# PEER block of a transformer kernel on one Trainium2 core: the first two weighted activations made ready under the last block of U

## The chip, the cores and the metric

The kernel runs on one NeuronCore of one Trainium2 chip. The metric is the device time of one execution in microseconds (us). Three timed runs of the kernel before gave 4199.46, 4199.56 and 4203.69 us: the median is 4199.56 us. The profile comes from a fourth execution.

## What is computed

Two layers of a two-stream trunk follow a first block. The change touches only the last part of each layer, a feed-forward block named PEER with 128 x 128 experts. It is called three times with 256 tokens: in layer 0 for both streams, in layer 1 for one. From the reference, cut:

```python
def peer_ffn(h, wq, sub_keys, eu, ev):
    ...
        q = (t @ wq).reshape(TOKEN_BLOCK, PEER_HEADS, 2, PEER_DK // 2)
        s = jnp.einsum("thpd,hpnd->thpn", q, sub_keys).astype(jnp.float32)
        st, it = lax.top_k(s, PEER_TOPK)
        ...
        best, pos = lax.top_k(cand, PEER_TOPK)
        e = jnp.take_along_axis(cidx, pos, axis=-1)
        g = jax.nn.softmax(best, axis=-1)
        u = jnp.take(eu, e, axis=0)
        act = jax.nn.gelu(jnp.einsum("thkd,td->thk", u, t).astype(jnp.float32), approximate=False)
        return jnp.einsum("thk,thkd->td", (g * act).astype(ev.dtype), jnp.take(ev, e, axis=0))
```

The kernel does not gather rows. It multiplies the tokens by all 16384 rows of `eu`, multiplies the result by a dense matrix of gates that is zero where an expert was not chosen, and multiplies that by all rows of `ev`.

## The kernel before

**Blocks and passes.** Weights come as blocks of 128 x 1024 numbers (512 KB). One call of PEER, a "pass" here, takes 8 blocks of `wq`, then 128 blocks of `eu` (U blocks, `u0 + c`), then 128 blocks of `ev` (V blocks, `v0 + c`), with c from 0 to 127. All blocks of the program come in one sequence through `ring`, which has NS = 4 places. SyncE starts the transfer of a block when the block four places earlier has been used: TensorE counts each block used in the semaphore `blocks_done`.

**Two parts of each number.** TensorE multiplies in a rounded format (fp32r), so each operand is split: the high part is its rounded copy, the low part the rest. For a block, ScalarE writes the high part (`high`, L1863, 128x1024, into `ring_hi`, 3 places) and then another engine the low part in the block's own place (`ring_lo`): GpSimd for U blocks below 48 (L1745), VectorE for the later U blocks (`low_up`, L2048) and for V blocks (`low`, L2063). A product takes three matmuls: high by high, high by low, low by high.

**U phase.** For U block c, `up` multiplies (24 matmuls of 256 columns, L1760 to L1762) into bank 4 + c % 4. ScalarE applies gelu (`gelu_late`, L1917 and L1919) and, behind it in the same function, writes the high part of the block that is three further: behind the gelu of U blocks 125, 126 and 127 it writes those of V blocks 0, 1 and 2. From c = 48 (`C0`) on, the gates are made beside this, four tokens at a time (a "quad", 64 of them): VectorE makes one-hot rows in `hotA` and `hotB` (L2019 to L2027), TensorE multiplies them (`build`, L1799) into banks 0 to 3, VectorE multiplies the rows of S that are there already (`gate`, L2036), and ScalarE stores the gates for the rows that are still to come (`keep_rest`, L1926); `gate_late` (L2042) multiplies such a row later. The last quad belongs to c = 126. S ends as the weighted activations, 128 rows of 128 x 256.

**V phase.** For each row c of S, ScalarE writes its high part (`weights`, L1938), VectorE its low part (`split`, L2056) and then the low part of V block c (`low`, L2063). `down` multiplies both (12 matmuls of 512 columns, L1813, L1815, L1817) into banks 0 to 3, where all 128 blocks add up. It waits for `v_lo` and `v_w`, which `low` and `split` count.

**Where the parts of S are kept.** `W_hi` and `W_lo` have four places each, in `H_r`. `H_r` also holds the high and low parts of the tokens, which every `up` reads. So nothing may be written there before the last U block has been multiplied: ScalarE and VectorE both wait for `blocks_done` at `n0 + v0`.

**Order.** Everything is written out by hand for each engine; each engine runs its instructions in that order, with semaphores between the engines. The loops of the V phase are hardware loops of 12 blocks a turn.

Of the kernel before, what the change touches and what calls it, by code (L numbers as in the profile page):

```python
# [9 lines left out]
F32R = mybir.dt.float32r  # L10
# [5 lines left out]
P = 128  # L16
D = 1024
KT = D // P
T = 256
# [13 lines left out]
PEER_H, TOPK, NK = 8, 16, 128  # L33
# [131 lines left out]
def build(nc, x, smalls, consts, mix_tables, tables, axial, w_in1, w_lru, w_br, w_o1, w_f1, w_f2, ada, w_in2,  # L165
          w_out2, w_q2, keys2, peer_u, peer_v, lam, out):
    ctx = ExitStack()
    with ctx:
# [3 lines left out]
        def pair_of(name, shape):  # L172

            at = (nc.sbuf_base + 31) // 32 * 32
            return sb(name, shape), nc.alloc_sbuf_tensor_at(name + "_r", shape, F32R, offset=at)
# [4 lines left out]
        H, H_r = pair_of("H", [P, KT, 2, T])  # L180
# [7 lines left out]
        arena_at = (nc.sbuf_base + 31) // 32 * 32  # L188
# [3 lines left out]
        blocks_done = ctx.enter_context(nc.semaphore("blocks_done"))  # L192
# [222 lines left out]
        A = Space(arena, n_arena)  # L415
# [64 lines left out]
        n0 = used[0]  # L480
# [80 lines left out]
        n0 = used[0]  # L561
# [132 lines left out]
        n0 = used[0]  # L694
# [109 lines left out]
        n0 = used[0]  # L804
# [116 lines left out]
        n0 = used[0]  # L921
# [70 lines left out]
        f = A.take(FFN_T, T)  # L992
        n0 = used[0]
# [58 lines left out]
        for l in range(LAYERS):  # L1052
# [85 lines left out]
            n0 = used[0]  # L1138
# [546 lines left out]
            for s in streams:  # L1685
# [3 lines left out]

                R = A.take(3, T)  # L1690
                S = A.take(NK, T)
                hotA = A.take(2, 4, P)
                hotB = A.take(2, 4, P)
                late = A.take(4, T)
                flat = S.rearrange("p c t -> p (c t)")
                work = Space(flat[:, 64 * T:], 64 * T)
# [11 lines left out]
                half = work.take(2, PEER_H, TOPK)  # L1708
                cand2 = S2.rearrange("p i k -> p (i k)").rearrange("p (h k) -> p h k", k=256)
                rows_, cols_, wts = (R[:, i, :] for i in range(3))  # L1710
                W_hi, W_lo = (H_r[:, 2 * i:2 * i + 2, :, :].rearrange("p a s t -> p (a s) t") for i in range(2))
                n0 = used[0]
                u0, v0 = 8, 8 + NK
                C0, QUADS = 48, T // 4
                first_row = [C0 + q * (NK - C0) // QUADS for q in range(QUADS)]

                def quads_at(c):

                    return [q for q in range(QUADS) if first_row[q] == c]

                def built(c):

                    return sum(f <= c for f in first_row)

                with Phase("keys_in", "by_q", "s_ps", "a_s", "v_read", "v_diff", "a_e", "v_found", "t_ps", "a_t",
# [5 lines left out]
                    def turns(it, n):  # L1731
                        return n if it is None else it * 12 + n
# [125 lines left out]
                    def _(act):  # L1858
                        def high(m, it=None):
                            arrived(act, n0 + m, None if it is None else it * 3)  # L1860
                            if m >= NH:
                                act.wait_ge(blocks_done, turns(it, n0 + m - NH + 1))
                            act.activation(ring_hi[:, m % NH, :], ring[:, (n0 + m) % NS, :], ACT.Copy).then_inc(a_hi, 1)  # L1863

                        def gelu(c, it=None):
                            act.wait_ge(blocks_done, turns(it, n0 + u0 + c + 1))
                            row = S[:, c, :] if it is None else S[:, bass.ds(it * 12 + c, 1), :].rearrange("p a t -> p (a t)")
                            act.activation(row, bank[4 + c % 4][:, 0:T], ACT.Gelu).then_inc(a_gelu, 1)
# [43 lines left out]
                        def gelu_late(c):  # L1912
                            t = 4 * built(c)
                            act.wait_ge(blocks_done, n0 + u0 + c + 1)
                            if c >= C0 + 4:
                                act.wait_ge(v_late, c - C0 - 3)
                            g = act.activation(late[:, c % 4, 0:t], bank[4 + c % 4][:, 0:t], ACT.Gelu)  # L1917
                            if t < T:
                                g = act.activation(S[:, c, t:], bank[4 + c % 4][:, t:T], ACT.Gelu)  # L1919
                            g.then_inc(a_gelu, 1)  # L1920
                            high(u0 + c + NH)

                        def keep_rest(q):
                            act.wait_ge(v_g, q + 1)
                            f = first_row[q]
                            act.activation(S[:, f:, 4 * q:4 * q + 4],  # L1926
                                           bank[q % 4][:, :].rearrange("p (t k) -> p k t", t=4)[:, f:, :],
                                           ACT.Copy).then_inc(a_rest, 1)

                        for c in range(C0, NK):  # L1930
                            gelu_late(c)
                            for q in quads_at(c):
                                keep_rest(q)
                        def weights(c, it=None):
                            if it is not None or c >= 4:
                                act.wait_ge(blocks_done, turns(it, n0 + v0 + c - 3))
                            w = S[:, c, :] if it is None else S[:, bass.ds(it * 12 + c, 1), :].rearrange("p a t -> p (a t)")
                            act.activation(W_hi[:, c % 4, :], w, ACT.Copy).then_inc(a_whi, 1)  # L1938

                        act.wait_ge(blocks_done, n0 + v0)  # L1940
                        act.wait_ge(v_g, QUADS)
                        act.wait_ge(v_late, NK - C0)
                        weights(0)
                        weights(1)
                        with act.Fori(0, 10) as it:
                            for c in range(12):
                                weights(2 + c, it)
# [7 lines left out]
                    def _(dve):  # L1955
# [27 lines left out]
                        for n in range(TT):  # L1983
                            dve.wait_ge(a_s, 4 * (n + 1))
                            cand = SC[n].rearrange("p i k -> p (i k)").rearrange("p (h k) -> p h k", k=256)
                            t, f = top[n], found[n]
# [43 lines left out]
                        def gate(q):  # L2030
                            f = first_row[q]
                            dve.wait_ge(g_ps, q + 1)
                            dve.wait_ge(a_gelu, f)
                            w = S[:, 0:f, 4 * q:4 * q + 4]
                            o = bank[q % 4][:, :].rearrange("p (t k) -> p k t", t=4)[:, 0:f, :]
                            dve.tensor_tensor(w, w, o, ALU.mult).then_inc(v_g, 1)  # L2036

                        def gate_late(c):
                            t = 4 * built(c)
                            dve.wait_ge(a_gelu, c + 1)  # L2040
                            dve.wait_ge(a_rest, built(c))
                            dve.tensor_tensor(S[:, c, 0:t], S[:, c, 0:t], late[:, c % 4, 0:t], ALU.mult).then_inc(v_late, 1)  # L2042
# [8 lines left out]
                        def split(c, it=None):  # L2051
                            if it is not None or c >= 4:
                                dve.wait_ge(blocks_done, turns(it, n0 + v0 + c - 3))
                            w = S[:, c, :] if it is None else S[:, bass.ds(it * 12 + c, 1), :].rearrange("p a t -> p (a t)")
                            dve.wait_ge(a_whi, turns(it, c + 1))
                            dve.tensor_tensor(W_lo[:, c % 4, :], w, W_hi[:, c % 4, :].bitcast(F32),  # L2056
                                              ALU.subtract).then_inc(v_w, 1)

                        def low(c, it=None):
                            m = v0 + c  # L2060
                            dve.wait_ge(a_hi, turns(it, m + 1))
                            slot = (n0 + m) % NS
                            dve.tensor_tensor(ring_lo[:, slot, :], ring[:, slot, :], ring_hi[:, m % NH, :].bitcast(F32),  # L2063
                                              ALU.subtract).then_inc(v_lo, 1)
# [7 lines left out]
                        for c in range(C0, NK):  # L2072
                            quads = quads_at(c)
                            for q in quads:
                                gate(q)
                                if q + 2 < QUADS:
                                    hit_keys(q + 2)
                            if c + 2 < NK:
                                low_up(c + 2)
                            for q in quads:  # L2080
                                if q + 2 < QUADS:
                                    weigh_keys(q + 2)
                            if c > C0:
                                gate_late(c - 1)
                        gate_late(NK - 1)
                        dve.wait_ge(blocks_done, n0 + v0)

                        with dve.Fori(0, 10) as it:
                            for c in range(12):
                                split(c, it)  # L2090
                                low(c, it)
                        for c in range(120, NK):
                            split(c)
                            low(c)
                used[0] += 8 + 2 * NK
# [157 lines left out]
```

## Time and profile before

| | |
|---|---|
| median of three runs | 4199.56 us |
| time of the profiled execution | 4205.55 us |
| its span, first to last instruction | 4201.9 us |
| mean granted TensorE clock over the span | 0.949 of full |
| TensorE matmul busy | 3852.6 us (92%) |
| VectorE busy | 2364.2 us (56%) |
| ScalarE busy | 1688.7 us (40%) |
| GpSimd busy | 782.0 us (19%) |

Busy time is time with an instruction running; the granted clock is the share of TensorE's full clock that the chip let through. Between span and time of the same execution lie 3.65 us that have no instruction. In the rows further below, times count from the first instruction.

### The profile page before, as it was taken

How to read it: one execution, taken by the hardware profiler on the slowest of the kernel's cores; microseconds unless marked ns; L12 is line 12 of the kernel's file. 1: busy time of each engine (PE TensorE's matmuls, PEld its weight loads, DVE VectorE, ACT ScalarE, POOL GpSimd, SP SyncE). 2: the span in 40 equal slices, each digit the busy share in tenths (PEclk: the TensorE clock that was granted, in tenths of full speed). 3: DMA queues.
4: the chain of work that ended last, by engine and by line, in shares of the span. 5: the costliest groups of instructions: out<-in, count | busy, mean ns of one | idle time of the engine just before them, and what ended most of it. 6: DMA issues, size and time to landing. Idle time of an engine off the chain costs nothing. (4 is left out here: it accounts for less than half of the span.)

```text
span 4201.9 us, 67550 instructions
## 1 busy us (share of the span) xinstructions
PE 3852.6 (92%) x23930; PEld 3376.7 (80%) x23930; DVE 2364.2 (56%) x4653; ACT 1688.7 (40%) x2999; POOL 782.0 (19%) x315
## 2 busy tenths in 40 slices
PE   7997788978978999999989999999879799999998
PEld 7984378966655999988879999888767699998887
DVE  5002322226451878965547889655555377896555
ACT  3542202313332544444545444454433244444544
POOL 5750004600002830000018400000000085000000
PEclk9997899998889999999999999999988899999999
DMA  5565644632102544456645545566421154445664
GB/s 185 177 200 179 210 153 135 179 107 76 59 1 79 162 146 149 148 167 193 193 152 165 150 146 146 165 192 193 151 83 52 54 164 150 150 147 161 193 192 150
DMA packets 168448, 614.95 MB, mean 146 GB/s; under 512 B 18592, under 2 KB 20000, under 8 KB 167968
## 3 DMA queue, kind: packets, MB, share of 16 engines
q1 hardware_dynamic: 168224, 611.88, 47.7%
q8 instruction: 150, 2.46, 0.2%
q14 instruction: 74, 0.61, 0.0%
HBM read 610.76 MB, written 1.05 MB: 146 GB/s over the span
## 5 line engine op out<-in xcount | busy, mean ns | idle before, releaser
L1863 ACT ACTIVATE ring_hi<-ring 128x1024 fp32r<-128x1024 f32 x792 | 839.3, 1060 | 616.2 <-DMA ring<-in_peer_v 510.2
L1760 PE MATMUL bank<-H_r,ring_hi 128*128 128x256 f32 x3264 | 947.5, 290 | 64.3 <-POOL ring_r L1745 62.8
L1761 PE MATMUL bank<-H_r,ring_hi 128*128 128x256 f32 x3264 | 927.2, 284 | 0.0
L1762 PE MATMUL bank<-H_r,ring_r 128*128 128x256 f32 x3264 | 926.6, 284 | 0.0
L1745 POOL TENSOR_TENSOR ring_r<-ring,ring_hi 128x1024 fp32r<-128x1024 f32 x168 | 456.1, 2729 | 1429.3 <-ACT ring_hi L1863 1428.6
L1760 PEld LDWEIGHTS bank<-H_r,ring_hi 128*128 128x128 f32 x3264 | 629.8, 193 | 72.3 <-POOL ring_r L1745 46.4
L1761 PEld LDWEIGHTS bank<-H_r,ring_hi 128*128 128x128 f32 x3264 | 630.5, 193 | 0.0
L1762 PEld LDWEIGHTS bank<-H_r,ring_r 128*128 128x128 f32 x3264 | 629.5, 193 | 0.0
L1813 PE MATMUL bank<-ring_hi,H_r 128*128 128x512 f32 x1536 | 476.6, 392 | 12.2 <-DVE ring_r L2063 12.1
L1815 PE MATMUL bank<-ring_r,H_r 128*128 128x512 f32 x1536 | 475.5, 391 | 0.0
L1817 PE MATMUL bank<-ring_hi,H_r 128*128 128x512 f32 x1536 | 475.5, 391 | 0.0
L2063 DVE TENSOR_TENSOR ring_r<-ring,ring_hi 128x1024 fp32r<-128x1024 f32 x384 | 467.9, 1219 | 0.0
L290 PE MATMUL bank<-H_r,ring_hi 128*128 128x256 f32 (+1 forms) x1464 | 457.9, 313 | 0.0
L2056 DVE TENSOR_TENSOR H_r<-arena,H_r 128x256 fp32r<-128x256 f32 x384 | 163.4, 426 | 452.4 <-ACT H_r L1938 441.1
L280 POOL TENSOR_TENSOR ring_r<-ring,ring_hi 128x1024 fp32r<-128x1024 f32 x133 | 318.9, 2401 | 503.0 <-ACT ring_hi L274 502.3
L1813 PEld LDWEIGHTS bank<-ring_hi,H_r 128*128 128x128 f32 x1536 | 290.0, 189 | 73.8 <-DVE ring_r L2063 13.6
L1815 PEld LDWEIGHTS bank<-ring_r,H_r 128*128 128x128 f32 x1536 | 290.1, 189 | 60.6
L1817 PEld LDWEIGHTS bank<-ring_hi,H_r 128*128 128x128 f32 x1536 | 290.0, 189 | 60.7
L289 PE MATMUL bank<-H_r,ring_hi 128*128 128x256 f32 x1064 | 305.0, 287 | 28.7 <-POOL ring_r L280 28.7
L2048 DVE TENSOR_TENSOR ring_r<-ring,ring_hi 128x1024 fp32r<-128x1024 f32 x240 | 293.1, 1221 | 65.6 <-ACT ring_hi L1863 64.5
L291 PE MATMUL bank<-H_r,ring_r 128*128 128x256 f32 x1064 | 304.0, 286 | 0.0
L290 PEld LDWEIGHTS bank<-H_r,ring_hi 128*128 128x128 f32 x1464 | 289.8, 198 | 14.2
(318 smaller groups left out, 5300.1 us busy)
## 6 DMA issues: line engine op xcount, KB each, us to landing
ring<-in_peer_u SPq DMA_DIRECT2D x384, 512.0 KB, 3.6
ring<-in_peer_v SPq DMA_DIRECT2D x384, 512.0 KB, 3.6
ring<-in_w_in SPq DMA_DIRECT2D x135, 512.0 KB, 3.6
ring<-in_ada SPq DMA_DIRECT2D x96, 512.0 KB, 4.7
ring<-in_w_f SPq DMA_DIRECT2D x72, 512.0 KB, 3.7
ring<-in_w_br SPq DMA_DIRECT2D x24, 512.0 KB, 3.6
ring<-in_w_q SPq DMA_DIRECT2D x24, 512.0 KB, 3.6
ring<-in_w_out SPq DMA_DIRECT2D x16, 512.0 KB, 3.6
```

Of the source, the lines that this page charges most:

```text
L280: eng.tensor_tensor(ring_lo[:, slot, :], ring[:, slot, :], ring_hi[:, m % NH, :].bitcast(F32), ALU.subtract).then_inc(lows, 1)
L289: pe.matmul(o, hi[:, k], x_hi(kt), start=(kt == 0), stop=False)
L290: pe.matmul(o, hi[:, k], x_lo(kt), start=False, stop=False)
L1745: pool.tensor_tensor(ring_lo[:, slot, :], ring[:, slot, :], ring_hi[:, m % NH, :].bitcast(F32), ALU.subtract).then_inc(p_lo, 1)
L1760: pe.matmul(o, hi[:, k], x_hi_[:, kt, :], start=(kt == 0), stop=False)
L1761: pe.matmul(o, hi[:, k], x_lo_[:, kt, :], start=False, stop=False)
L1762: mm = pe.matmul(o, lo[:, k], x_hi_[:, kt, :], start=False, stop=(kt == KT - 1))
L1813: pe.matmul(bank[2 * t + e][:, :], w_hi, hi[:, v], start=start, stop=False)
L1815: pe.matmul(bank[2 * t + e][:, :], w_hi, lo[:, v], start=False, stop=False)
L1817: mm = pe.matmul(bank[2 * t + e][:, :], w_lo, hi[:, v], start=False, stop=stop)
L1863: act.activation(ring_hi[:, m % NH, :], ring[:, (n0 + m) % NS, :], ACT.Copy).then_inc(a_hi, 1)
L2063: dve.tensor_tensor(ring_lo[:, slot, :], ring[:, slot, :], ring_hi[:, m % NH, :].bitcast(F32), ALU.subtract).then_inc(v_lo, 1)
```

## The change

`W_hi` and `W_lo` move from `H_r` to the place in `arena` where `hotA` and `hotB` lie (2 x 1024 numbers a partition, the same size as 2 x 4 x 256). The one-hot rows are no longer needed once the last quad has been multiplied and gated. ScalarE writes the high parts of rows 0 and 1 ahead of the gelu of U block 127, behind a wait for `g_ps` and `v_g` at 64. VectorE writes the low parts of rows 0 and 1 and of V blocks 0 and 1 ahead of `gate_late(127)`. The waits for `blocks_done` at `n0 + v0` on both engines are gone. VectorE's loop then runs over c from 2 to 13 in its first turn.

```diff
                 S = A.take(NK, T)
+                W_hi, W_lo = (nc.alloc_sbuf_tensor_at(f"w_{part}{l}{s}", [P, 4, T], F32R,
+                                                      offset=arena_at + 4 * (A.at + i * 4 * T))
+                              for i, part in enumerate(("high", "low")))
                 hotA = A.take(2, 4, P)
                 hotB = A.take(2, 4, P)
...
-                W_hi, W_lo = (H_r[:, 2 * i:2 * i + 2, :, :].rearrange("p a s t -> p (a s) t") for i in range(2))
...
-                        for c in range(C0, NK):
-                            gelu_late(c)
-                            for q in quads_at(c):
-                                keep_rest(q)
                         def weights(c, it=None):
...
-                        act.wait_ge(blocks_done, n0 + v0)
-                        act.wait_ge(v_g, QUADS)
+                        for c in range(C0, NK):
+                            if c == NK - 1:
+                                act.wait_ge(g_ps, QUADS)
+                                act.wait_ge(v_g, QUADS)
+                                weights(0)
+                                weights(1)
+                            gelu_late(c)
+                            for q in quads_at(c):
+                                keep_rest(q)
                         act.wait_ge(v_late, NK - C0)
-                        weights(0)
-                        weights(1)
                         with act.Fori(0, 10) as it:
...
                             if c > C0:
                                 gate_late(c - 1)
+                        for c in range(2):
+                            split(c)
+                            low(c)
                         gate_late(NK - 1)
-                        dve.wait_ge(blocks_done, n0 + v0)
 
                         with dve.Fori(0, 10) as it:
-                            for c in range(12):
+                            for c in range(2, 14):
                                 split(c, it)
                                 low(c, it)
-                        for c in range(120, NK):
+                        for c in range(122, NK):
                             split(c)
                             low(c)
```

In the changed kernel the line numbers are a few off those of before. ScalarE, end of the U phase in the first pass, before: the gelu of U block 126 (from bank6), the high part of V block 1, the last `keep_rest` (bank3), the gelu of U block 127 (bank7), the high part of V block 2, `weights` of rows 0 and 1, and the loop's first instructions, which are row 2.

```order
L1917 ACTIVATE arena<-bank6 128x256
L1863 ACTIVATE ring_hi<-ring 128x1024
L1926 ACTIVATE arena<-bank3 128x2x4
L1917 ACTIVATE arena<-bank7 128x256
L1863 ACTIVATE ring_hi<-ring 128x1024
L1938 ACTIVATE H_r_50<-arena 128x256 x2
L1945 UNCONDITIONAL_BRANCH
```

The same place of the changed kernel:

```order
L1919 ACTIVATE arena<-bank6 128x256
L1865 ACTIVATE ring_hi<-ring 128x1024
L1928 ACTIVATE arena<-bank3 128x2x4
L1936 ACTIVATE w_high00_10652<-arena 128x256 x2
L1919 ACTIVATE arena<-bank7 128x256
L1865 ACTIVATE ring_hi<-ring 128x1024
L1948 UNCONDITIONAL_BRANCH
```

Two `weights` moved ahead of the last gelu and of the high part of V block 2. VectorE, the same place, before: the last `gate`, then `gate_late` of rows 125, 126 and 127, the loop, and in it `split(0)` and `low(0)`.

```order
L2036 TENSOR_TENSOR arena<-arena,bank3 128x126x4
L2042 TENSOR_TENSOR arena<-arena 128x252
L2042 TENSOR_TENSOR arena<-arena 128x256 x2
L2088 UNCONDITIONAL_BRANCH
L2088 ISA
L2055 REGISTER_ALU
L2056 ISA
L2056 TENSOR_TENSOR H_r_50<-arena,H_r_50 128x256
L2061 REGISTER_ALU
L2063 TENSOR_TENSOR ring_r_49<-ring,ring_hi 128x1024
```

The changed kernel, from `gate_late` of row 125 on:

```order
L2045 TENSOR_TENSOR arena<-arena 128x252
L2045 TENSOR_TENSOR arena<-arena 128x256
L2059 TENSOR_TENSOR w_low00_10653<-arena,w_high00_10652 128x256
L2066 TENSOR_TENSOR ring_r_49<-ring,ring_hi 128x1024
L2059 TENSOR_TENSOR w_low00_10653<-arena,w_high00_10652 128x256
L2066 TENSOR_TENSOR ring_r_49<-ring,ring_hi 128x1024
L2045 TENSOR_TENSOR arena<-arena 128x256
L2093 UNCONDITIONAL_BRANCH
```

Two pairs of `split` and `low` moved out of the loop and ahead of `gate_late(127)`. TensorE, GpSimd and SyncE have the same instructions in the same order as before.

## Rows read from the trace of the kernel before

**Rows 1.** The page's costliest groups: first matmul of `down`, busy, mean, idle before.

```profile
L1813 PE MATMUL bank<-ring_hi,H_r 128*128 128x512 f32 x1536 | 476.6, 392 | 12.2 <-DVE ring_r L2063 12.1
```

**Rows 2.** Timeline of PE, pass 1: start, duration, what, [idle before <-releaser].

```profile
1818.05 1.22 PE L1813 MATMUL bank<-ring_hi,H_r 128*128 128x512 f32 x2 [3.93 <-DVE ring_r L2063]
...
1826.10 0.61 PE L1813 MATMUL bank<-ring_hi,H_r 128*128 128x512 f32 x2
...
1828.82 0.61 PE L1813 MATMUL bank<-ring_hi,H_r 128*128 128x512 f32 x2
```

**Rows 3.** Timeline of ACT, pass 1, around the end of the U phase.

```profile
1812.13 1.06 ACT L1863 ACTIVATE ring_hi<-ring 128x1024 fp32r<-128x1024 f32 x1 [0.46 <-DMA ring<-in_peer_v]
1813.09 0.16 ACT L1926 ACTIVATE arena<-bank 128x8 f32<-128x8 f32 x1
...
1815.89 1.01 ACT L1938 ACTIVATE H_r<-arena 128x256 fp32r<-128x256 f32 x3
```

**Rows 4.** Timeline of DVE, the same stretch.

```profile
1813.35 0.43 DVE L2042 TENSOR_TENSOR arena<-arena 128x256 f32<-128x256 f32 x1 [3.84 <-ACT arena L1926]
...
1816.44 0.43 DVE L2056 TENSOR_TENSOR H_r<-arena,H_r 128x256 fp32r<-128x256 f32 x1 [1.44 <-ACT H_r L1938]
1816.78 1.22 DVE L2063 TENSOR_TENSOR ring_r<-ring,ring_hi 128x1024 fp32r<-128x1024 f32 x1
```

**Rows 5.** Timeline of PE, passes 2 and 3: first matmuls of V blocks 0 and 2.

```profile
2668.08 1.22 PE L1813 MATMUL bank<-ring_hi,H_r 128*128 128x512 f32 x2 [4.01 <-DVE ring_r L2063]
...
2676.11 0.61 PE L1813 MATMUL bank<-ring_hi,H_r 128*128 128x512 f32 x2
...
3827.79 1.22 PE L1813 MATMUL bank<-ring_hi,H_r 128*128 128x512 f32 x2 [3.87 <-DVE ring_r L2063]
...
3836.17 0.62 PE L1813 MATMUL bank<-ring_hi,H_r 128*128 128x512 f32 x2
```

**Rows 6.** Timeline of ACT, passes 2 and 3: the last `keep_rest`.

```profile
2662.46 0.17 ACT L1926 ACTIVATE arena<-bank 128x8 f32<-128x8 f32 x1
...
3822.31 0.17 ACT L1926 ACTIVATE arena<-bank 128x8 f32<-128x8 f32 x1
```

**Rows 7.** Timeline of DVE, passes 2 and 3: `gate_late(126)` and `split(0)` of each.

```profile
2662.73 0.42 DVE L2042 TENSOR_TENSOR arena<-arena 128x256 f32<-128x256 f32 x1 [3.28 <-ACT arena L1926]
...
2666.47 0.43 DVE L2056 TENSOR_TENSOR H_r<-arena,H_r 128x256 fp32r<-128x256 f32 x1 [1.52 <-ACT H_r L1938]
...
3822.58 0.42 DVE L2042 TENSOR_TENSOR arena<-arena 128x256 f32<-128x256 f32 x1 [3.25 <-ACT arena L1926]
...
3826.17 0.43 DVE L2056 TENSOR_TENSOR H_r<-arena,H_r 128x256 fp32r<-128x256 f32 x1 [1.37 <-ACT H_r L1938]
```

**Rows 8.** Stretches: length; busy of PE, PEld, DVE, ACT, POOL; clock, DMA share, GB/s.

```profile
1425.00:1515.00 90.00, 83.77 (x686) 82.38 (x685) 72.16 (x214) 45.45 (x64) 80.28 (x30) 1.00 0.55 163
1818.05:1823.38 5.33, 5.33 (x13) 4.17 (x14) 2.89 (x4) 0.00 (x0) 0.00 (x0) 0.50 0.01 2
1823.38:2169.00 345.62, 345.56 (x1525) 285.76 (x1523) 195.06 (x250) 170.72 (x250) 0.00 (x0) 1.00 0.64 192
3130.70:3134.10 3.40, 3.40 (x19) 3.40 (x18) 1.78 (x5) 0.00 (x0) 0.00 (x0) 0.50 0.09 36
```

**Rows 9.** Waits of PE, 1425 to 1515: total, times, longest.

```profile
PE bank L1760 <- POOL ring_r L1745: 6.2, 7, 1.3
```

**Rows 10.** Timeline of PE at two other gaps.

```profile
3129.87 0.63 PE L1177 MATMUL bank<-CS,arena 128*128 128x128 f32 x4 [2.00 <-ACT arena L1225]
...
3877.43 0.73 PE L1813 MATMUL bank<-ring_hi,H_r 128*128 128x512 f32 x2 [0.30 <-DVE ring_r L2063]
```

**Rows 11.** Timeline of DVE, pass 1: low part of V block 5.

```profile
1832.03 1.22 DVE L2063 TENSOR_TENSOR ring_r<-ring,ring_hi 128x1024 fp32r<-128x1024 f32 x1
```

**Rows 12.** Weight loads by line: duration min/median/max in ns; `down` and `build`.

```profile
L1813 PEld LDWEIGHTS bank<-ring_hi,H_r x1536: 186/188/333, 1818.1 to 4178.1; 128*128 128x128 f32 x192
L1799 PEld LDWEIGHTS bank<-arena x1536: 186/192/338, 1524.9 to 3817.8; 128*128 128x128 f32 x192
```

## Prediction

> **What bounds the kernel now.** I read the page first: TensorE is busy nearly all the time, so only places where it stands still, or where its clock is low, can be worth anything. The group of the first matmul of `down` shows 12.2 us of idle time ahead of it, almost all of it waiting for VectorE's low part of a block, 12.1 us [rows 1]. The timeline of PE says where that is: once at each change from U to V, 3.93, 4.01 and 3.87 us [rows 2, 5], with 0.30 us left for one hiccup in the third V phase [rows 10]. Next, how long a V block takes: block 1 starts to be followed by block 2 at 1826.10 and block 3 at 1828.82, so 2.72 us a block [rows 2]. But the first two V blocks of pass 1 took from 1818.05 to 1826.10, 8.05 us where two blocks should take 5.44. The windows say why: the granted clock was 0.50 from 1818.05 to 1823.38, that is 1.2 GHz, and 1.00 (2.4 GHz) from there on to the end of the pass [rows 8]. So each change of phase costs twice: the standstill, and a V block at half clock behind it.
>
> Why the standstill lasts 3.9 us is read from the timelines of ACT and DVE. The last U block's matmuls end at 1818.05 - 3.93 = 1814.12. Only then do the last gelu and the high part of V block 2 run; the `weights` start at 1815.89 [rows 3], `split(0)` at 1816.44, `low(0)` at 1816.78, and PE goes on at 1818.05 [rows 4, 2]. From `weights` to `split` is 0.55 us, from `split` to PE 1.61 us. None of this needs the last U block except for the place it writes to. ScalarE's last `keep_rest` starts at 1813.09 and VectorE's `gate_late(126)` at 1813.35, behind it [rows 3, 4]: from there on both are free.
>
> **The change part by part.** Nothing is added or taken away but the two waits. Three passes, and in each two `weights`, two `split` and two `low` move to the front.
>
> *The new start of V.* In pass 1 `keep_rest` runs from 1813.09 for 0.16 us. I let `weights(0)` start 0.11 behind its start, since each engine's next instruction begins some 0.05 to 0.1 us ahead of the end of the last (the high part of V block 1 from 1812.13 for 1.06 us, `keep_rest` at 1813.09 [rows 3]). That is 1813.20, and `split(0)` 0.55 later is 1813.75; `gate_late(126)`, ahead of it on VectorE, is just over by then (1813.35 + 0.43). `split(0)` stood at 1816.44, so it comes 2.69 us earlier, and PE with it: 1815.36 in place of 1818.05. Pass 2: `keep_rest` 2662.46 [rows 6], `weights(0)` 2662.57, `split(0)` 2663.12 where `gate_late(126)` (2662.73 + 0.42) ends too; it stood at 2666.47 [rows 7], 3.35 us. Pass 3: 3822.31, 3822.42, 3822.97, against 3826.17: 3.20 us. Together 9.24 us. Left are standstills of 3.93 - 2.69 = 1.24, 4.01 - 3.35 = 0.66 and 3.87 - 3.20 = 0.67 us. Pass 1 keeps more because `keep_rest` stands there behind the high part of V block 1, which waited for its DMA until 1812.13 [rows 3].
>
> *The clock.* The trace has no standstill of this kind at this place, so I bound it. From below: in 1425 to 1515, also under U blocks, PE stood still seven times for GpSimd, 6.2 us in all and up to 1.3 us at a time [rows 9], and the granted clock was 1.00 throughout [rows 8]. From above: a standstill of 2.00 us ended at 3129.87 [rows 10], and the clock was 0.50 from 3130.7 to 3134.1 [rows 8]. My 1.24, 0.66 and 0.67 us lie under 1.3, the first of them closely, so I take it that the clock holds in all three. What comes back is the excess of the first two V blocks over 5.44 us: 8.05 - 5.44 = 2.61 in pass 1, 2676.11 - 2668.08 - 5.44 = 2.59 in pass 2, 3836.17 - 3827.79 - 5.44 = 2.94 in pass 3 [rows 2, 5]: 8.14 us.
>
> The Trainium skill, TensorE: Matmul & The Clock Gate, section "Part 1: The HAM clock gate", says that the count of matmuls at the low clock after a pause varies between runs of one kernel (6, 11 or 14 were seen), since the monitor is not tied to the kernel. Here the trace shows some 12 to 13 a time. By that rule, at 0.2 us a matmul, three places would hold 3.6 to 8.4 us in the timed runs and not 8.14 for certain, and the sum would be 12.8 to 17.6 us, an estimate from that page.
>
> *ScalarE's new wait.* `weights(0)` waits for the last quad's product and gate, and the gelu of U block 127 is queued behind it. `keep_rest`, one instruction ahead, waits for the same gate already, so the wait costs nothing; and two `weights` of about 0.34 us each (three took 1.01 [rows 3]) are over at 1813.9, before the last U block ends at 1814.12. No cost.
>
> *VectorE's new order.* `gate_late(127)`, and behind it `weights(2)` and `split(2)`, now stand behind two `low`. From the start of `low(0)` PE is 1.27 us away (1816.78 to 1818.05 [rows 2, 4]). VectorE needs 1.22 + 0.43 + 1.22 + 0.43 = 3.30 us to the end of `gate_late(127)`, about 0.15 to hand over, 0.55 from `weights(2)` to `split(2)`, and 1.61 to PE: 6.61, or 5.34 us after PE starts V block 0. Counted in whole durations, with no overlap, that is still ahead of 5.44, when PE comes to V block 2; with the overlaps of 0.1 us an instruction it is about 0.5 us ahead. No cost, but the cover is thin: a delay past it is paid in full.
>
> *The ring.* The pause used to let V block 3 land. It is still asked for when the last U block ends, and PE comes to it 0.66 + 3 x 2.72 = 8.8 us later. Block 4 is asked for when block 0 is done, as in the steady phase, where the low part of V block 5 is ready at 1832.03 + 1.22 = 1833.25 [rows 11] and PE comes to it at 1828.82 + 2 x 2.72 = 1834.26: 1.0 us to spare. The transfers keep the DMA engines busy 0.64 of the time at 192 GB/s [rows 8], so the V phase runs at TensorE's pace and an earlier start becomes an earlier end. The one late transfer in the third V phase cost 0.30 us [rows 10].
>
> *Sum.* 9.24 + 8.14 = 17.4 us, three changes of phase together. The profiled execution would take 4205.55 - 17.4 = 4188.2 us. The median of the runs stands 6.0 us under that execution (4199.56); I take the same saving there: 4182.2, so 4182 us.
>
> **The rivals.**
> *A, the pause goes, the half clock stays.* The clock could still fall behind 1.24 us, or behind the shorter ones; the timeline has nothing between 1.3 and 2.00 to tell, and other standstills of up to 1.3 us held. Then only 9.24 us come back: 4190.3 us. If it falls in pass 1 alone, 4184.8.
> *B, the wait moves on.* PE waits at V block 2 for the longer queue on VectorE, or later for the ring, and the half clock follows there. Against it: 0.5 to 1.0 us of cover. It must lose over 9 us in three passes to hide the gain, 3 us each: a wait of about 0.5 us and a slow block of 2.6 us each time. About 4191 to 4199, say 4196 us.
> *C, slower: the new place of the parts costs TensorE.* In the V phase it loads its weights from `arena`, where ScalarE and VectorE read and write too. There are 3 x 1536 = 4608 such loads. If each matmul took 3.8 ns more, the gain would be gone (17.4 / 4608); from 5.6 ns on the kernel is slower by 0.2%. The rows have a load from `arena` at 192 ns in `build` against 188 ns from `H_r` in `down` [rows 12]: 4 ns more. But a matmul is started every 227 ns (2.72 / 12), which covers a load of 192. With 8 ns exposed it would cost 36.9 - 17.4 = 19.5 us: 4219 us.
> *D, nothing happens,* because something on ScalarE or VectorE still ends after the last U block. The order of the changed kernel speaks against it: `split(0)` and `low(0)` stand ahead of all that needs that block.
>
> **How the numbers follow.** Forecast, both parts come back: 0.77. A, in part or whole: 0.12. B and D: 0.07. C: 0.04. Time of the likeliest: 4182. Downward the range takes in standstills gone to nothing (11.81 + 8.14 = 19.95 us, 4179.6) and some 1.5 us of scatter: 4178. Upward it takes in all of A: 4191. That leaves 1 in 10 out above. The likeliest alone has 4179 to 4186. A measurement of this kernel can tell about 0.2% from no change, 8.4 us. The forecast and two thirds of A are beyond that, for 9.24 is close to it: faster 0.85. The rest of A with B and D: same 0.11. C: slower 0.04.
>
> **What the profile of the changed kernel would show.** At each change from U to V a gap of 0.6 to 1.3 us ahead of the first matmul of `down`, in place of 3.9; `weights` twice between the last `keep_rest` and the last gelu; pairs of first V blocks in 5.4 us, not 8; granted clock 1.00 across the change. Against me would be: the clock at 0.50 behind the short gap (A), a wait of `down` for VectorE at V block 2 (B), matmuls of `down` over 227 ns apart (C), or `weights(0)` after the last U block (D). The likeliest error is in the clock of pass 1.

## The result, and the profile after

The changed kernel is slower: 4215.27 us median against 4203.16 us for the kernel before over 13 runs each, a ratio of 1.0031 with a 95% interval from 1.0022 to 1.0039. Forecast was 4182 us. The profiled execution took 4217.31 us with a span of 4213.8 us; before it was 4205.55 and 4201.9.

At the change from U to V everything went as forecast. Timeline of PE in the changed kernel, the first matmuls of `down` in the three passes (L1815 is the line that was L1813, answering to [rows 2, 5]); the second and third rows are the first matmuls of V blocks 1 and 2 of pass 1:

```profile
1810.48 0.74 PE L1815 MATMUL bank<-ring_hi,w_high 128*128 128x512 f32 x2 [1.05 <-DVE ring_r L2066]
...
1813.39 0.63 PE L1815 MATMUL bank<-ring_hi,w_high 128*128 128x512 f32 x2
...
1816.19 0.63 PE L1815 MATMUL bank<-ring_hi,w_high 128*128 128x512 f32 x2
...
2669.28 0.73 PE L1815 MATMUL bank<-ring_hi,w_high 128*128 128x512 f32 x2 [0.61 <-DVE ring_r L2066]
...
3833.59 0.74 PE L1815 MATMUL bank<-ring_hi,w_high 128*128 128x512 f32 x2 [0.61 <-DVE ring_r L2066]
```

The standstills are 1.05, 0.61 and 0.61 us, 2.27 in place of 11.81. V block 0 runs from 1810.48 to 1813.39, 2.91 us, and with block 1 it takes 5.71 us to 1816.19, where before the two took 8.05 us in pass 1, 5.33 of them at half clock [rows 2, 8]. Windows of 8 us across the three changes of phase show the clock at 1.00:

```profile
1808.00:1816.00 8.00, 6.95 (x36) 5.71 (x36) 5.80 (x10) 4.27 (x9) 0.00 (x0) 1.00 0.53 155
2667.00:2675.00 8.00, 7.39 (x39) 6.10 (x39) 5.47 (x9) 4.07 (x9) 0.00 (x0) 1.00 0.56 172
3831.00:3839.00 8.00, 7.39 (x40) 6.19 (x39) 5.58 (x9) 4.38 (x9) 0.00 (x0) 1.00 0.59 160
```
ACT (ScalarE) and then DVE (VectorE), the same stretch, answering to [rows 3, 4]:

```profile
1808.27 0.16 ACT L1928 ACTIVATE arena<-bank 128x8 f32<-128x8 f32 x1
1808.32 0.71 ACT L1936 ACTIVATE w_high<-arena 128x256 fp32r<-128x256 f32 x2
1809.47 0.38 ACT L1919 ACTIVATE arena<-bank 128x256 f32<-128x256 f32 x1 [0.43 <-PE bank L1764]
```

```profile
1808.53 0.43 DVE L2045 TENSOR_TENSOR arena<-arena 128x256 f32<-128x256 f32 x1 [3.71 <-ACT arena L1928]
1808.87 0.42 DVE L2059 TENSOR_TENSOR w_low<-arena,w_high 128x256 fp32r<-128x256 f32 x1
1809.21 1.22 DVE L2066 TENSOR_TENSOR ring_r<-ring,ring_hi 128x1024 fp32r<-128x1024 f32 x1
...
1811.81 0.42 DVE L2045 TENSOR_TENSOR arena<-arena 128x256 f32<-128x256 f32 x1
1813.11 0.42 DVE L2059 TENSOR_TENSOR w_low<-arena,w_high 128x256 fp32r<-128x256 f32 x1 [0.88 <-ACT w_high L1936]
1813.45 1.22 DVE L2066 TENSOR_TENSOR ring_r<-ring,ring_hi 128x1024 fp32r<-128x1024 f32 x1
```

Both `weights` are over before the last gelu; `low(0)` ends at 1810.43 and PE starts. The low part of V block 2 is over at 1814.67; PE comes to it at 1816.19.

The loss is in what looks like no event at all. Windows of the steady phases, kernel before and then the changed kernel: the first row lies in the V phase of pass 1, the second in the U phase. In the V phase every PE instruction is a matmul of `down`, so length over count is the step from one to the next.

```profile
1850.00:2140.00 290.00, 290.00 (x1281) 240.14 (x1280) 166.50 (x214) 145.25 (x215) 0.00 (x0) 1.00 0.64 193
1600.00:1790.00 190.00, 190.00 (x1614) 190.00 (x1614) 172.92 (x277) 82.84 (x202) 0.00 (x0) 1.00 0.48 148
```

```profile
1850.00:2140.00 290.00, 290.00 (x1244) 233.48 (x1243) 162.27 (x208) 140.78 (x207) 0.00 (x0) 1.00 0.62 187
1600.00:1790.00 190.00, 190.00 (x1613) 190.00 (x1613) 173.10 (x277) 82.84 (x202) 0.00 (x0) 1.00 0.49 147
```

PE is busy 100%, the clock is 1.00 and PE waits for nothing, in both. But 290 us hold 1281 matmuls before and 1244 after: 226.4 against 233.1 ns (both some 0.3 ns low, since a matmul that reaches over an edge is counted whole). The U phase has not changed (1614 and 1613 instructions in 190 us). No matmul record is missing: the page counts all 1536 of each line of `down`, before and after. The page says the same in its mean duration and hides it well:

```profile
L1815 PE MATMUL bank<-ring_hi,w_high 128*128 128x512 f32 x1536 | 483.8, 396 | 2.8 <-DVE ring_r L2066 2.5
```

The wait went from 12.2 to 2.8 us [rows 1], the mean duration from 392 to 396 ns, although 392 had three V blocks at half clock in it. At 6.7 ns for each of 3 x 1536 = 4608 matmuls the V phases lose 30.9 us. With 9.5 us of standstill and 8.1 us of half clock won, that is 13.3 us more; the spans differ by 11.9 and the medians by 12.1. The close fit is in part chance: in the profiled execution of the changed kernel the first U block started 5.2 us earlier (1335.6 against 1340.8 us), and the three U phases took some 4 us longer, though the change touches neither.

### The profile page after: what moved, and what is told of

Read it like the earlier page. It is cut to its first block and busy times, and to the rows that moved or that the text cites. A ratio compares the mean times of both kernels' runs of the same rounds, so it can differ in the third digit from the quotient of the medians.

```text
span 4213.8 us, 67544 instructions
## 1 busy us (share of the span) xinstructions
PE 3872.1 (92%) x23930; PEld 3369.8 (80%) x23930; DVE 2369.5 (56%) x4653; ACT 1689.5 (40%) x2999; POOL 781.0 (19%) x315
## 3 DMA queue, kind: packets, MB, share of 16 engines
HBM read 610.76 MB, written 1.05 MB: 145 GB/s over the span
## 5 line engine op out<-in xcount | busy, mean ns | idle before, releaser
L1762 PE MATMUL bank<-H_r,ring_hi 128*128 128x256 f32 x3264 | 948.4, 291 | 65.7 <-POOL ring_r L1747 64.6
L1764 PE MATMUL bank<-H_r,ring_r 128*128 128x256 f32 x3264 | 927.3, 284 | 0.0
L1762 PEld LDWEIGHTS bank<-H_r,ring_hi 128*128 128x128 f32 x3264 | 630.6, 193 | 73.7 <-POOL ring_r L1747 46.4
L1764 PEld LDWEIGHTS bank<-H_r,ring_r 128*128 128x128 f32 x3264 | 629.9, 193 | 0.0
L1815 PE MATMUL bank<-ring_hi,w_high 128*128 128x512 f32 x1536 | 483.8, 396 | 2.8 <-DVE ring_r L2066 2.5
L1817 PE MATMUL bank<-ring_r,w_high 128*128 128x512 f32 x1536 | 482.9, 395 | 0.0
L1819 PE MATMUL bank<-ring_hi,w_low 128*128 128x512 f32 x1536 | 482.9, 395 | 0.0
L2059 DVE TENSOR_TENSOR w_low<-arena,w_high 128x256 fp32r<-128x256 f32 x384 | 163.4, 426 | 469.4 <-ACT w_high L1936 469.4
L1815 PEld LDWEIGHTS bank<-ring_hi,w_high 128*128 128x128 f32 x1536 | 288.2, 188 | 74.0 <-DVE ring_r L2066 5.0
L1819 PEld LDWEIGHTS bank<-ring_hi,w_low 128*128 128x128 f32 x1536 | 288.8, 188 | 69.8
L1817 PEld LDWEIGHTS bank<-ring_r,w_high 128*128 128x128 f32 x1536 | 288.8, 188 | 69.5
```

What stands on the lines that cost most here:

```text
L1762: pe.matmul(o, hi[:, k], x_hi_[:, kt, :], start=(kt == 0), stop=False)
L1764: mm = pe.matmul(o, lo[:, k], x_hi_[:, kt, :], start=False, stop=(kt == KT - 1))
L1815: pe.matmul(bank[2 * t + e][:, :], w_hi, hi[:, v], start=start, stop=False)
L1817: pe.matmul(bank[2 * t + e][:, :], w_hi, lo[:, v], start=False, stop=False)
L1819: mm = pe.matmul(bank[2 * t + e][:, :], w_lo, hi[:, v], start=False, stop=stop)
```

## The experiments

**place_only.** The placing alone: the kernel before with the parts where the changed kernel has them, order and waits as they were.

```diff
                 S = A.take(NK, T)
+                W_hi, W_lo = (nc.alloc_sbuf_tensor_at(f"w_{part}{l}{s}", [P, 4, T], F32R,
+                                                      offset=arena_at + 4 * (A.at + i * 4 * T))
+                              for i, part in enumerate(("high", "low")))
                 hotA = A.take(2, 4, P)
...
-                W_hi, W_lo = (H_r[:, 2 * i:2 * i + 2, :, :].rearrange("p a s t -> p (a s) t") for i in range(2))
```

> The kernel before, its order and its waits untouched; only W_hi and W_lo lie in arena, at the place where the changed kernel has them. Theory P (the place alone slows the matmuls of down): the step from one matmul of down to the next is 231 to 236 ns instead of 227, some 10 us a pass and 31 us in all, on top of the old standstills: about 4234 us against 4203. Rival T (the matmuls are slower because of the new order: engines now work at other times beside TensorE): steps stay at 227 ns and the time is that of before, 4203 us.

Measured: 4240.23 us against 4205.57, ratio 1.0081 (1.0055 to 1.0106). Window of the V phase of pass 1:

```profile
1850.00:2140.00 290.00, 290.00 (x1245) 233.65 (x1244) 162.24 (x208) 141.26 (x208) 0.00 (x0) 1.00 0.63 187
```

290 / 1245 = 232.9 ns. The place makes the step from one matmul of `down` to the next longer, with the old order of all engines. Rival T, the new order as the cause, has fallen.

**first_two.** The order nearly alone: the changed kernel, with only rows 0 and 1 in `arena`. From row 2 on the parts are in `H_r` again, so ScalarE's wait for the last U block comes back, but behind the last gelu.

```diff
-                W_hi, W_lo = (nc.alloc_sbuf_tensor_at(f"w_{part}{l}{s}", [P, 4, T], F32R,
...
+                W_first = [nc.alloc_sbuf_tensor_at(f"w_{part}{l}{s}", [P, 2, T], F32R,
+                                                   offset=arena_at + 4 * (A.at + i * 4 * T))
+                           for i, part in enumerate(("high", "low"))]
+                W_rest = [H_r[:, 2 * i:2 * i + 2, :, :].rearrange("p a s t -> p (a s) t") for i in range(2)]
+
+                def part_of(i, c, it=None):
+                    return W_first[i][:, c, :] if it is None and c < 2 else W_rest[i][:, c % 4, :]
...
                         act.wait_ge(v_late, NK - C0)
+                        act.wait_ge(blocks_done, n0 + v0)
```

> The changed kernel, but only rows 0 and 1 have their parts in arena; from row 2 on they lie in H_r as in the kernel before, written after the last U block is done. Under any of the theories of place (P1, P2) all but two V blocks a pass run at 227 ns and the short standstill stays: 4203 - 9.9 - 8.1, about 4185 us. Under T the steps stay at 231 to 236 ns and it takes about 4215 us.

Measured: 4184.11 us, ratio 0.9954 (0.9937 to 0.9970). Two changes of phase in the timeline of PE, and the window:

```profile
1821.84 0.73 PE L1820 MATMUL bank<-ring_hi,w_high 128*128 128x512 f32 x2 [0.95 <-DVE ring_r L2072]
...
2668.97 0.73 PE L1820 MATMUL bank<-ring_hi,w_high 128*128 128x512 f32 x2 [0.61 <-DVE ring_r L2072]
```

```profile
2720.00:2980.00 260.00, 260.00 (x1149) 215.29 (x1148) 148.91 (x192) 130.67 (x192) 0.00 (x0) 1.00 0.65 193
```

260 / 1149 = 226.3 ns, short standstills, 21 us less than before. So the two halves of the change can be had apart, and the half that the forecast was about is worth about what it said.

**h_plus64.** What is it about the place? `W_hi` and `W_lo` in the memory of `H`, 64 bytes further on. The kernel is otherwise that of before.

```diff
...
+            places[name] = at
...
-                W_hi, W_lo = (H_r[:, 2 * i:2 * i + 2, :, :].rearrange("p a s t -> p (a s) t") for i in range(2))
+                W_hi, W_lo = (nc.alloc_sbuf_tensor_at(f"w_{part}{l}{s}", [P, 4, T], F32R,
+                                                      offset=places["H"] + 64 + 4 * i * 4 * T)
+                              for i, part in enumerate(("high", "low")))
```

> The kernel before, with W_hi and W_lo still in the memory of H, but 64 bytes further: H begins at byte 61568 of a partition, a multiple of 128, while the place in arena is byte 216768, which is 64 past a multiple of 128. Theory P1 (it is the start address modulo 128): steps of 231 to 236 ns here too, about 4234 us. Rival P2 (it is the region, arena against H, or what else is read and written there): steps of 227 ns, 4203 us.

**after_plus64.** The changed kernel with the parts 64 bytes further on, `late` too.

```diff
-        n_arena = 36612
+        n_arena = 36624
...
-                                                      offset=arena_at + 4 * (A.at + i * 4 * T))
+                                                      offset=arena_at + 64 + 4 * (A.at + i * 4 * T))
...
                 hotB = A.take(2, 4, P)
+                A.take(16)
```

> The changed kernel with W_hi and W_lo 64 bytes further, at byte 216832, a multiple of 128; late moves up by the same 64 bytes. Theory P1: steps return to 227 ns, the V phases lose their 31 us, and the time is 4215 - 31 = 4184 us. Rival P2: nothing changes, 4215 us.

Measured: h_plus64 4232.84 us, ratio 1.0067 (1.0042 to 1.0091); after_plus64 4215.77 us, 1.0027 (1.0013 to 1.0041). Windows, h_plus64 first:

```profile
1850.00:2140.00 290.00, 290.00 (x1244) 233.52 (x1243) 161.80 (x208) 141.08 (x208) 0.00 (x0) 1.00 0.63 188
```

```profile
1850.00:2140.00 290.00, 290.00 (x1245) 233.18 (x1244) 161.34 (x208) 141.75 (x208) 0.00 (x0) 1.00 0.64 188
```

Both are slow, 233.1 and 232.9 ns. P2, the region as the cause, falls by the first, for nothing but 64 bytes was changed; P1, the address modulo 128, falls by the second, at a multiple of 128 that should have been fast. The addresses (bytes in a partition; those of the ring counted back from `H` by the sizes of the tensors) suggested the next question: `ring` 16512, `ring_hi` 32896 and `H` 61568 are alike modulo 4096, and with them the parts of before; the slow places 216768, 216832 and 61632 are not like them modulo 256, nor modulo 512.

**sweep_a, sweep_b, sweep_c.** The edit of h_plus64 with another shift in each pass, (128, 256, 512), (32, 384, 2048) and (96, 160, 224).

> The kernel before, W_hi and W_lo in the memory of H, another shift in each pass: 128, 256 and 512 bytes. With a shift of 0 the step of down is 227 ns, with 64 bytes it was 233 on average, and at the place in arena (192 past a multiple of 512, as H plus 64) it was 233 with the same alternation of 231 and 236. Theory M (what counts is the start address modulo 512, the length of the 128 numbers that one weight load reads): 128 and 256 bytes are slow, above 230 ns, 512 bytes is fast, 227 ns. Rival N (any tensor that isn't H_r itself is slow, whatever its address): all three passes are slow. Rival K (modulo 128): all three are fast.

> The same with shifts of 32, 384 and 2048 bytes. Theory M: 32 and 384 are slow, above 230 ns a step, 2048 is fast, 227 ns. Rival N: all slow. Rival K: only 32 is slow.

> The kernel before, W_hi and W_lo in the memory of H shifted by 96, 160 and 224 bytes in passes 1, 2 and 3. Theory M2 says all three are slow, 232 to 233 ns a step, since only multiples of 256 have been fast (0, 256, 512, 2048) and 32, 64, 128 and 384 slow. A theory by which only distances of 32 to 128 cost would have 224 near 227 ns.

Windows of the V phases of passes 1, 2 and 3, of sweep_a, sweep_b and sweep_c in turn:

```profile
1850.00:2140.00 290.00, 290.00 (x1250) 235.15 (x1249) 162.53 (x209) 142.02 (x208) 0.00 (x0) 1.00 0.61 188
2720.00:2980.00 260.00, 260.00 (x1149) 215.29 (x1148) 149.74 (x192) 130.56 (x191) 0.00 (x0) 1.00 0.64 192
3880.00:4130.00 250.00, 250.00 (x1104) 207.01 (x1103) 143.66 (x184) 125.56 (x184) 0.00 (x0) 1.00 0.63 193
```

```profile
1850.00:2140.00 290.00, 290.00 (x1244) 233.50 (x1244) 161.17 (x208) 141.94 (x208) 0.00 (x0) 1.00 0.61 187
2720.00:2980.00 260.00, 260.00 (x1120) 210.83 (x1119) 145.31 (x187) 127.44 (x188) 0.00 (x0) 1.00 0.62 188
3880.00:4130.00 250.00, 250.00 (x1101) 205.88 (x1100) 143.48 (x184) 124.80 (x183) 0.00 (x0) 1.00 0.64 192
```

```profile
1850.00:2140.00 290.00, 290.00 (x1240) 233.63 (x1239) 161.30 (x208) 140.76 (x206) 0.00 (x0) 1.00 0.61 187
2720.00:2980.00 260.00, 260.00 (x1116) 209.31 (x1115) 144.62 (x186) 127.00 (x186) 0.00 (x0) 1.00 0.61 187
3880.00:4130.00 250.00, 250.00 (x1073) 201.28 (x1072) 138.70 (x179) 121.54 (x178) 0.00 (x0) 1.00 0.63 187
```

Length over count gives, by shift in bytes:

| shift | 0 | 32 | 64 | 96 | 128 | 160 | 224 | 256 | 384 | 512 | 2048 |
|---|---|---|---|---|---|---|---|---|---|---|---|
| ns a step | 226.4 | 233.1 | 233.1 | 233.9 | 232.0 | 233.0 | 233.0 | 226.3 | 232.1 | 226.4 | 227.1 |

Each of these kernels was timed once: 4217.36, 4219.41 and 4236.91 us, with one, two and three slow passes. Of the shifts tried, the multiples of 256 are fast and no other is. N (any other tensor is slow) and K (modulo 128) have fallen. M (modulo 512) put 256 among the slow ones and missed; the period is 256 bytes.

**all_plus64.** The kernel before, with everything 64 bytes later.

```diff
+        pad = sb("pad", [P, 16])
         ring, ring_lo = pair_of("ring", [P, NS, SLOT])
```

> The kernel before with 64 bytes of padding ahead of ring, so that ring, ring_hi and H (with W_hi and W_lo in it) all begin 64 bytes later. Theory M in its relative form (what counts is where the stationary operand lies against the moving one, modulo 512): down keeps 227 ns a step and the time is that of before, about 4204 us. In its absolute form (128 past a multiple of 512 is the good address): 233 ns and some 31 us more.

One run: 4207.46 us, against 4205.53 for the kernel before. 290 us of the V phase hold 1281 matmuls, as before:

```profile
1850.00:2140.00 290.00, 290.00 (x1281) 240.22 (x1280) 166.11 (x214) 145.74 (x214) 0.00 (x0) 1.00 0.63 193
```

So it is a distance between tensors and not an address in itself.

**ring_apart.** The same padding between `ring` and `ring_hi`, so that `ring` alone is 64 bytes off; `arena` moves with `H`.

> The kernel before with 64 bytes of padding between ring and ring_hi, so that ring_hi and H (with W_hi and W_lo) begin 192 past a multiple of 256 while ring, with the low parts of the blocks, stays at 128. Theory M2 (TensorE is slow while its stationary and its moving operand differ in their start address modulo 256): of the 12 matmuls of a V block the four with the low part of the block (middle line) are slow, some 233 ns a step, the eight with ring_hi keep 227: about 229 ns on average, 10 us more in three passes; in the U phase the steps at the low part of the block become slower too, if that phase feels it at all. Rival S (what counts is where W lies against S in arena, which ScalarE and VectorE read meanwhile): nothing changes against the kernel before, since H and arena move together: 227 ns in all steps.

One run: 4201.69 us, beside 4209.72 for one run of the kernel before. Windows of the V and the U phase of pass 1, then the lines of `down` in the first of them (duration min/median/max in ns; 389 in all three before):

```profile
1850.00:2140.00 290.00, 290.00 (x1257) 235.92 (x1256) 163.79 (x210) 142.16 (x210) 0.00 (x0) 1.00 0.63 189
1600.00:1790.00 190.00, 190.00 (x1634) 190.00 (x1633) 174.25 (x279) 84.02 (x205) 0.00 (x0) 1.00 0.49 149
```

```profile
L1814 PE MATMUL bank<-ring_hi,H_r x419: 388/390/396, 1850.1 to 2139.9; 128*128 128x512 f32 x140
L1816 PE MATMUL bank<-ring_r,H_r x418: 393/394/395, 1850.6 to 2139.2; 128*128 128x512 f32 x140
L1818 PE MATMUL bank<-ring_hi,H_r x420: 387/393/398, 1849.7 to 2139.7; 128*128 128x512 f32 x140
```

290 / 1257 = 230.7 ns: slower, though the distance from `W` (`W_hi` and `W_lo`) to the weighted activations is unchanged. Rival S has fallen, and the distance to `ring` counts. But M2 was too simple. It had 229 ns, with the two lines of `ring_hi` untouched; many of their matmuls are longer too, up to 396 and 398. The slow matmul is not told by its own two operands alone. And the U phase got faster: 1634 instructions in 190 us, where all other kernels so far had 1612 to 1615.

**arena_first.** The changed kernel, with `arena` allocated right behind `H` and the small tensors behind `arena`, so that `W_hi` begins at 212096, like `ring` modulo 256.

```diff
         H, H_r = pair_of("H", [P, KT, 2, T])
+        n_arena = 36612
+        arena_at = (nc.sbuf_base + 31) // 32 * 32
+        arena = sb("arena", [P, n_arena])
...
-        n_arena = 36612
...
-        arena_at = (nc.sbuf_base + 31) // 32 * 32
-        arena = sb("arena", [P, n_arena])
```

> The changed kernel, but arena is laid right behind H and the small tensors behind arena: hotA, and with it W_hi, then begins at byte 212096, 128 past a multiple of 512, as ring, ring_hi and H do. Nothing else differs. Theory M: down runs at 227 ns and the time is 4215 - 31 = 4184 us, as much as when only the first two rows lie in arena. Rival N, or a theory by which reads and writes of arena by other engines cost TensorE: 233 ns, 4215 us. Other phases may shift by a few us either way, since their tensors in arena move too.

Measured: 4186.54 us against 4205.53, ratio 0.9952 (0.9939 to 0.9964).

```profile
1850.00:2140.00 290.00, 290.00 (x1281) 240.15 (x1280) 166.32 (x213) 145.86 (x214) 0.00 (x0) 1.00 0.64 193
```

226.4 ns, with the parts in `arena` throughout and as far from the weighted activations as in the changed kernel. Reads and writes of `arena` by the other engines cost TensorE nothing that shows.

**h_apart64, h_apart128.** Since ring_apart had sped up the U phase: arena_first with `H`, which holds the tokens' parts, moved alone by 64 or 128 bytes; `arena` moves by 256 bytes in all, so that `W` stays like `ring` modulo 256. The edit for 64 bytes, against arena_first; for 128 both paddings are 32 numbers.

```diff
+        pad = sb("pad", [P, 16])
         H, H_r = pair_of("H", [P, KT, 2, T])
+        pad2 = sb("pad2", [P, 48])
```

> arena_first with H alone 64 bytes further; W_hi, W_lo, ring and ring_hi stay alike modulo 256. In ring_apart, where ring lay 64 bytes off ring_hi and H, a V block was slower but the steps of the U phase fell from 119.7 to 118.3 ns. Theory U1 (any distance between TensorE's operands costs, in U as in V; ring_apart was a chance): the U phase gets slower than 119.7, the V phase stays at 227, time above 4187. Theory U2 (with 256 columns, where the next weights are loaded in almost the whole step, a distance helps): U steps of 118 ns or less, V at 227, some 13 us less than arena_first, 4174 us.

> The same with H 128 bytes further, half of 256. U1: U steps above 119.7 ns, time above 4187. U2: below, about 4174 us.

Measured: h_apart64 4159.07 us against 4199.61, ratio 0.9909 (0.9879 to 0.9938); h_apart128 4179.38, 0.9941 (0.9918 to 0.9964). Windows of V (pass 2) and U (pass 1), h_apart64 and then h_apart128:

```profile
2720.00:2980.00 260.00, 260.00 (x1149) 215.37 (x1148) 149.28 (x192) 130.21 (x192) 0.00 (x0) 1.00 0.65 193
1600.00:1790.00 190.00, 190.00 (x1634) 190.00 (x1633) 174.31 (x279) 83.88 (x205) 0.00 (x0) 1.00 0.51 149
```

```profile
2720.00:2980.00 260.00, 260.00 (x1149) 215.29 (x1148) 148.70 (x192) 130.55 (x192) 0.00 (x0) 1.00 0.65 193
1600.00:1790.00 190.00, 190.00 (x1609) 190.00 (x1608) 172.39 (x277) 82.09 (x201) 0.00 (x0) 1.00 0.49 147
```

The V phase is as fast as before. (Counted from the starts in the traces, a step of `up` is 119.8 ns before and 117.8 in ring_apart, where the expectation has 119.7 and 118.3.) At 64 bytes the window of the U phase holds 1634 in place of 1612 to 1615 instructions; at 128 it holds 1609, a little slower. U2 is right for 64, though more was won than its 13 us. At 128 neither is right: the window is no faster, against U2, but the time did not rise above 4187 us, against U1, and by its interval it can't be told from arena_first.

h_apart64 is the fastest of all, 4159 us, and by the ratios it lies 0.43%, some 18 us, under arena_first. From the first to the last start of the first line of `up` (L1762 and L1764), the traces have in pass 1 472.7 us for arena_first (1345.4 to 1818.1) and 466.8 for h_apart64 (1330.4 to 1797.2), the 8 blocks of `wq` included; in pass 2 it is 473.9 and 465.2, in pass 3 472.8 and 465.9. That is 21.5 us less in three passes, so the U phases alone can account for the 18. At 128 bytes the same stretches are together within 2 us of arena_first. Products of other phases also read `ring` against `H`; their share was not taken apart.

## Why the prediction was wrong

*The standstill.* Right. Forecast 1.24, 0.66 and 0.67 us left, measured 1.05, 0.61, 0.61; won 9.5 us for 9.24. In pass 1 `keep_rest` stood 1.16 us ahead of the end of the U phase and not 1.03 as before (1809.43 - 1808.27, 1814.12 - 1813.09), which is most of the difference. The time that the saving was taken from was 3.6 us low: the median of the first three runs, 4199.56, against 4203.16 of thirteen. That alone would not have left the range.

*The clock.* Right. It stayed at 1.00 in all three passes. The first two V blocks of pass 1 took 5.71 us where two blocks at the new step take 5.60; so nearly all of the 8.14 us came back. The prediction takes 6, 11 and 14 matmuls at the low clock from the section "Part 1: The HAM clock gate" of the Trainium skill's page "TensorE: Matmul & The Clock Gate"; the page gives these counts for the start of a kernel, not for a pause inside one. The eight kernels here with the old order have 24 such pauses at the change from U to V, of 3.7 to 4.9 us, and behind every one 8 to 14 matmuls of `down` ran at half clock. first_two has both terms without the third and lies 21 us under the kernel before where the sum was 17.4; its interval, 0.30% to 0.63%, holds that sum.

*ScalarE's wait, VectorE's order, the ring.* Right: no cost that shows. VectorE had 1.5 us to spare at V block 2 where I had counted 0.1 to 0.5, so B had nothing to stand on.

*The place.* Here it failed. The step was under rival C: "a matmul is started every 227 ns, which covers a load of 192". I priced the new place by how long a weight load lasts, found 4 ns in the row of another line, and let the matmul hide it. Neither is what happened. The loads are as long as before, a median of 188 ns in all three lines of `down`, as this pair shows for the middle one, before and after (1850 to 2140):

```profile
L1815 PEld LDWEIGHTS bank<-ring_r,H_r x426: 187/188/188, 1850.8 to 2139.4; 128*128 128x128 f32 x142
```

```profile
L1817 PEld LDWEIGHTS bank<-ring_r,w_high x414: 187/188/192, 1850.4 to 2139.2; 128*128 128x128 f32 x138
```

What grew is the step of the matmul itself, by 6.7 ns, past the 5.6 ns from which C decides. C was the right rival with the right break-even, at a chance of 0.04 that a load's duration could not justify: I had no row for a matmul whose operands lie at another distance, and took a row about something else for a bound. In the main sum the place had no term at all.

*What is shown and what is open.* Shown: the place and not the order costs the 31 us (place_only, first_two). Within `down` it is where `W` lies, modulo 256 bytes, against the blocks in `ring` and `ring_hi`: with all three alike the step is 226 to 227 ns (before, sweeps, all_plus64, arena_first), and it is longer at every other distance tried. ring_apart, where `ring` differs from both others, does not tell whether it is `ring` against `W` or against `ring_hi` that costs. Not shown is the mechanism: why 512 columns want distance 0 while the U phase with 256 columns is faster at 64, or why in ring_apart matmuls are touched whose own operands are alike. At 64 bytes in h_plus64 the starts of `down` in the trace lie by turns some 231 and some 236 ns apart, in all three lines alike, where before all lie 226 or 227 apart. That weights for one matmul are loaded while the one ahead still streams would fit a cost that falls on a neighbour, but no run here tells it.

## What to carry to other kernels

Moving a buffer is an edit with a price of its own, even at equal size, type and reader: look up its start address against that of TensorE's other operand, and test the move alone, apart from the reordering that it is meant to allow. The distances that were fast here are measured for these two shapes of matmul only. A loss spread over thousands of matmuls shows in no wait and no busy share; divide a steady window's length by its count of matmuls, before and after. Where only the first few blocks need the new place, give it to those alone, as first_two does.

## What the hardware showed that was not expected

- The step of a 512-column fp32r matmul was 226 to 227 ns with both operands alike modulo 256 bytes, and 232 to 234 ns at distances of 32, 64, 96, 128, 160, 224 and 384 bytes: 3% of TensorE's time at full clock, no wait in sight.
- The U phase (256 columns, weights from the ring) goes another way: 190 us held 1612 to 1615 instructions with the tokens' parts and the ring at distance 0, 1634 at 64 bytes and 1609 at 128. With 64 bytes the whole kernel came to 4159 us, 0.9% under the kernel before, from two paddings and an order of allocation beside the change itself.
- At the change from U to V, 18 standstills of TensorE of 0.6 to 1.1 us (six kernels) left its granted clock at 1.00, 2.4 GHz, every time; 24 of 3.7 to 4.9 us (eight kernels) were each followed by a stretch at 0.50, 1.2 GHz, that held 8 to 14 matmuls of `down`.
